# Turning blocks of 128x128 by fp32 products with the identity instead of transpose mode, in the samples' attention and the first two query tiles

## What is computed

```python
# compressed, selected and window branch, each a softmax over its keys
s = jnp.einsum('btghd,bkgd->bghtk', q, k) * scale + bias
p = jax.nn.softmax(jnp.where(ok, s, NEG), axis=-1)
o = jnp.einsum('bghtk,bkgd->btghd', p, v)
# merged by sigmoid gates, multiplied by the gate path, then projected
y = concat([o_merged * silu(z_nsa), u * mix * silu(z_g)]) @ w_out
```

## Time and profile before

| what | value |
|---|---|
| median of 3 runs | 1179.73 us (1175.66 to 1183.05) |
| the profiled execution | 1175.34 us, its span 1173.6 us |
| mean granted TensorE clock | 0.96 |
| PE busy | 1081.7 us (92%) |
| DVE busy | 587.2 us (50%) |
| ACT busy | 442.8 us (38%) |

### The profile page before, as it was taken

The page is one execution under the profiler, slowest core; times in us unless marked ns, Lnnn a source line. Parts: engine busy times, 40 slices in busy tenths (PEclk is TensorE's granted clock), DMA queues, the critical chain, the costliest instruction groups (busy, mean ns, idle before and its releaser), DMA issues. The chain is left out here.

```text
span 1173.6 us, 15483 instructions
## 1 busy us (share of the span) xinstructions
PE 1081.7 (92%) x6041; PEld 936.9 (80%) x6041; DVE 587.2 (50%) x1093; ACT 442.8 (38%) x746; POOL 191.0 (16%) x259
## 2 busy tenths in 40 slices
PE   6999999999998788889888789999899999998996
PEld 5879879999996676777777676887788889996884
DVE  4534221133233577777877436344689995215322
ACT  4330121110034466676666403222276675214211
POOL 2210578000003232221100000001021220000110
PEclk9999999999997899999999956999999999998999
DMA  8451002121122000000010711222311111401221
GB/s 286 129 192 59 19 5 59 37 54 37 37 78 101 1 1 1 1 1 1 1 48 26 238 50 55 93 90 91 95 36 37 37 36 51 165 1 59 87 93 63
DMA packets 64566, 74.81 MB, mean 64 GB/s; under 512 B 13794, under 2 KB 48658, under 8 KB 64495
## 3 DMA queue, kind: packets, MB, share of 16 engines
q1 hardware_dynamic: 61902, 70.77, 19.0%
q0 software_dynamic: 2496, 3.04, 0.8%
q10 hardware_dynamic: 96, 0.03, 0.0%
HBM read 62.19 MB, written 16.34 MB: 67 GB/s over the span
## 5 line engine op out<-in xcount | busy, mean ns | idle before, releaser
L1301 PE MATMUL ps<-h1T_hi,w_c_hl 128*128 128x352 f32 x768 | 150.0, 325 | 12.9 <-ACT region_w L1244 8.7
L1301 PE MATMUL ps<-hT_hi,w_fm_hl 128*128 128x352 f32 x768 | 145.5, 324 | 0.8 <-ACT region_w L1093 0.8
L1301 PEld LDWEIGHTS ps<-h1T_hi,w_c_hl 128*128 128x128 f32 x768 | 128.0, 188 | 17.7 <-ACT region_w L1244 13.2
L1305 PE MATMUL ps<-ident,region_w 128*128 128x128 f32 (+2 forms) x730 | 116.9, 289 | 27.0 <-ACT region_w L1143 17.6
L1305 PEld LDWEIGHTS ps<-ident,region_w 128*128 128x128 f32 (+2 forms) x730 | 94.1, 149 | 53.1 <-DVE p_hl L2008 23.8
L1301 PEld LDWEIGHTS ps<-hT_hi,w_fm_hl 128*128 128x128 f32 x768 | 127.4, 188 | 1.3 <-issue 1.2
L2008 DVE TENSOR_TENSOR p_hl<-ps,p_hl 128x512 fp32r<-128x512 f32 x132 | 91.2, 691 | 72.9 <-ACT p_hl L1151 71.1
L1151 ACT CAST p_hl<-ps 128x512 fp32r<-128x512 f32 x132 | 77.2, 585 | 73.5 <-PE ps L1305 73.1
L1301 PE MATMUL ps<-p_hl,v_hl 128*128 128x512 f32 x264 | 95.4, 443 | 6.7 <-DVE p_hl L2008 3.4
L1143 ACT ACTIVATE region_w<-region_w,negm 128x640 f32<-128x640 f32 (+7 forms) x128 | 93.8, 735 | 5.5 <-DVE negm L1983 4.5
L1983 DVE CUSTOM_DVE_ANT_0 region_w<-ps,region_w 128x640 f32<-128x640 f32 (+7 forms) x128 | 88.0, 699 | 5.1 <-PE ps L1301 4.7
(11 more groups left out here) (278 smaller groups left out, 1823.1 us busy)
## 6 DMA issues: line engine op xcount, KB each, us to landing
region_w<-in_x_prompt SPq DMA_DIRECT2D x16, 512.0 KB, 3.6
region_w<-in_w_in_c SPq DMA_DIRECT2D x16, 512.0 KB, 3.9
region_w<-in_w_in_a SPq DMA_DIRECT2D x12, 512.0 KB, 3.8
rel_rows_dram<-rel_line_dram SPq DMA_DIRECT2D x8, 576.0 KB, 12.5
region_y<-in_w_in_a SPq DMA_DIRECT2D x8, 512.0 KB, 6.2
region_w<-rel_rows_dram SPq DMA_DIRECT2D x16, 256.0 KB, 4.8
region_w<-in_w_out_a SPq DMA_DIRECT2D x2, 2048.0 KB, 12.1
x_dram<-region_w SPq DMA_DIRECT2D x8, 512.0 KB, 2.6
```

The costliest lines, as they stand in the source:

```text
L1301: return nc.tensor.matmul(out, l, r, start=start, stop=stop, skip_group_check=True)
L1305: return nc.tensor.transpose(out, x, ident[0:k, 0:k])
```

## The change

A second helper turns a block by an ordinary fp32 product: the block is the stationary operand, as before, and the identity streams through. It takes the place of `flip` in all turns of the samples' keys, window keys and probabilities, and in the `turn` steps of query tiles 0 and 1. `turn_result`, `c_turn`, `out` and the turns of tiles 2 to 7 stay as they are. No instruction changes its place, no wait and no buffer changes.

```diff
+PRODUCT_TILES = 2
...
+            def turn_by_product(out, x):
+
+                k = x.shape[0]
+                return mm(out, x, ident[0:k, 0:k], True, True)
...
                     for c in range(HPG):
-                        m = flip(ps[:, 4 + k % 3, c * P:(c + 1) * P], probs[kind][:, c, b * P:(b + 1) * P])
+                        m = (turn_by_product if i < PRODUCT_TILES else flip)(
+                            ps[:, 4 + k % 3, c * P:(c + 1) * P], probs[kind][:, c, b * P:(b + 1) * P])
...
                 for j in range(2 * HALF):
-                    m = flip(ps[:, bank + j // 4, (j % 4) * P:(j % 4 + 1) * P], h.pages[:, j, 256:384])
+                    m = turn_by_product(ps[:, bank + j // 4, (j % 4) * P:(j % 4 + 1) * P], h.pages[:, j, 256:384])
...
                 for j in range(2 * HALF):
-                    flip(ps[:, bank + 2 + j // 4, (j % 4) * P:(j % 4 + 1) * P], h.wins[:, j, 0:P])
+                    turn_by_product(ps[:, bank + 2 + j // 4, (j % 4) * P:(j % 4 + 1) * P], h.wins[:, j, 0:P])
...
-                    flip(ps[:, bank + 1 + b, 0:P], buf[:, 0:P])
-                    flip(ps[:, bank + 1 + b, P:2 * P], buf[:, P:2 * P])
-                    flip(ps[0:NS, bank + 1 + b, 2 * P:3 * P], buf[:, PAST:PAST + NS])
-                return flip(ps[0:16, bank + 3, 0:P], h.logits_c)
+                    turn_by_product(ps[:, bank + 1 + b, 0:P], buf[:, 0:P])
+                    turn_by_product(ps[:, bank + 1 + b, P:2 * P], buf[:, P:2 * P])
+                    turn_by_product(ps[0:NS, bank + 1 + b, 2 * P:3 * P], buf[:, PAST:PAST + NS])
+                return turn_by_product(ps[0:16, bank + 3, 0:P], h.logits_c)
```

## The result

The changed kernel takes 1185.6 us in the median of 18 runs (1182.3 to 1190.97), the kernel before 1176.75 us in 18 runs (1170.74 to 1184.34). The ratio is 1.0073, with a 95% interval of 1.0054 to 1.0091: slower by 8.6 us (6.4 to 10.7). Forecast were 8.1 us more.

A forecast was written before the change was run, and what follows sets the result against it. PE bounds the samples but for one wait, and a ring of PE, ACT and DVE the tiles. Tiles +3.8 and samples +4.3 sum to +8.1 us, from 1179.73 to 1187.8; range 1174 to 1197.

The forecast's parts named there:

- The bound from the averages: Samples' averages, only 2 columns wide, take 0.42 us a product at 1.2 GHz: lower bound for the new product's price.
- Tiles: Turns of query tiles 0 and 1: +6.6 us on the path less 2.8 from the clock, +3.8 (bounds -2 to +9).
- the ring: In tiles 0 and 1 PE turns, ACT casts, DVE subtracts, PE waits 0.93 us; a later turn delays everything.
- the rise 7 us sooner: In tiles 0 and 1 the clock's rise at 384.3 comes some 7 us earlier, saving at most 2.8 us.
- Samples: Samples' attention: +7.3 us of longer turns on PE's path less 3.0 from the clock, +4.3 (bounds -8 to +10).
- first turns: The samples' first 24 turns, begun at the low clock level, end later as products: +2.9 us.
- the other eight: The samples' eight turns of the other half, with the clock falling or fallen: 3.3 us for 1.5, +1.5.
- The 14 products of the probabilities: Turns of the samples' probabilities at the low clock level: 14 x 0.21 = +2.9 us.
- The saving of 3 us in the values: Samples' value products partly run at 2.4 GHz after the probabilities' turns raise the clock: 3 of 8 us saved.
- The clock stays up: Rival: from first pages to output products, products keep or wake the high clock; about -15 us, 1164.5; chance 0.10.
- Nothing given back: Rival: in tiles and samples the clock does what it does now; +13.9 us, 1193.6; chance 0.25.
- Mostly hidden: Rival: more of the tiles' turn groups covered by PE's idle time; about +4 us, 1183.7; chance 0.15.

The follow-up runs named there:

- Measured alone: Against the kernel before, products only in the turns of query tiles 0 and 1, samples keeping transpositions: 1.0029, +3.4 us.
- all tiles: The change with products in the turns of all eight query tiles instead of two: 1.04, +47 us against the kernel before.
- samples alone: Against the kernel before, products only in the samples' attention, tiles keeping transpositions: 1.0016, +1.9 us.
- order: The change with each half's wide products of the probabilities made first and the narrow ones behind: 1.0055, +6.5 us against the kernel before.
- turned twice by transposition: The change with each of its 94 products replaced by two transpositions into the same place: 1.0033, +3.9 us against the kernel before.
- a gap filled by transpositions: The kernel before with 18 unused identity transpositions in PE's wait for the samples' exponentials: 0.9982.
- one filled by products: The kernel before with 9 unused fp32 identity products in PE's wait for the samples' exponentials: 0.9973.
- four fills together: The kernel before with PE's waits filled in four places by work with unused results: 0.9909, 1165.98 us.

## Why the prediction was right

The forecast was a price of +13.9 us, 5.8 of it given back by the clock, and so +8.1. Measured are +8.6; by the line through the runs of the kernel before, 12.4 of price and 3.7 given back (0.961 for 0.957). The mechanism holds: a product costs twice a transposition, most of that lies on the path, and a part comes back through the clock. Its level, 1187.8, was 2.2 us too high, since the median of the three runs it started from (1179.73) lies 3.0 us over that of the 18.

**The price of a product.** Foreseen 0.225 us at 2.4 GHz and 0.43 at 1.2 GHz; measured 0.20 and 0.425. The bound from the averages (0.42) was the right neighbour.

**Tiles.** Forecast +6.6 on the path less 2.8 of clock, +3.8. Measured alone +3.4 (0.7 to 6.2); at equal mean clock +6.6. That ACT's cast follows each turn was right: the ring got longer, and with all tiles four fifths of the price or more showed. By the forecast's own mark, the way to the first turn of tile 2, the change's profile grew by 8.4 us and not by 4, and the first low stretch got longer (23.9 us for 20.7) where it was to end sooner. About 5 of the 8.4 are price; the rest is 10 us more at the low level (37.5 for 27.3). So the rise 7 us sooner isn't how the clock gave something back in that execution. It came in one of six profiles with longer turns, and where in the tiles the runs gain their higher mean clock no profile shows.

**Samples.** Forecast +4.3; the profiled stage grew by 5.5, of which 0.4 came back in the first output; alone the part measured +1.9 (-1.1 to 4.9), and +7.7 at equal mean clock, where +7.3 was forecast without the clock. By terms: first turns +2.6 for +2.9, the other eight +1.7 for +1.5. The 14 products of the probabilities cost +4.5 and not +2.9, since in a product each change between a wide and a narrow stationary operand costs 0.45 us, which in a transposition it hardly does. The forecast had only the length of the records in this term. The saving of 3 us in the values had the right size and an uncertain place: it came there in "samples alone" (5.9 us for 9.2), in "order" and in "all tiles" (5.8 each); in the change's profile 2.9 us came at the second averages in its place, because the clock rose there.

**The rivals.** "The clock stays up" rested on a difference between the modes. The Trainium skill (TensorE: Matmul & The Clock Gate, Part 4: PE-mode transpose) says that the full clock doesn't engage for transpose mode, which doesn't count as busy time in the same way. That isn't borne out here for fp32 turns: turned twice by transposition the clock rose within 4.6 us of turns, and a gap filled by transpositions gave the same 2.4 GHz behind it as one filled by products (706.74 and 706.91). "Nothing given back", +13.9, is outside the measured interval. "Mostly hidden", about +4, is too, and the kernel with all tiles contradicts it. The total was near with help from errors that cancel, and that part is luck: the probabilities' price was 1.6 us too low, the tiles' clock came otherwise than told, and the prices of the two parts alone (6.6 and 7.7) add up to more than the whole's 12.4.

Still open: what decides when in an execution the clock changes. With it the way to tile 2 moves from 60.9 to 67.3 us for the same turns. I also didn't settle whether the stops at the width switches keep the clock low through the probabilities. For it: with fewer stops it rose during them, and the runs have a higher mean clock (0.964 for 0.961). Against it: with the same stops it rose at their end in "samples alone" and during them in "all tiles", where the 28 records took 6.5 us.

## What to carry to other kernels

Turning a block by an fp32 product costs twice a transposition at either clock, and no run here shows it to buy anything for the clock that transpositions of the same length don't. When the clock is low behind a wait, fill the wait itself with work whose result nobody reads, as long as it ends before the wait does: that costs nothing on the path, and here took 0.9% off with four fills together. Keep operands of one width together in a run of fp32 products. Before reading a difference of two profiles stage by stage, compare their mean clocks with those of the other runs: here the profile of the change was the slowest of 18, and nearly half of its +15.6 us was the clock.

## What the runs showed of the hardware that was not expected

- In fp32 products, alternating stationary operands of 128 and of 32 or 16 columns costs 0.45 us for each excursion at 1.2 GHz (1.73 us for six records instead of 1.28); grouping the widths took 0.45 off the half (3.87 to 3.42). Transpositions of the same widths kept 0.227 us each, where wide ones alone take 0.214.
- Work on the identity, with a result that is constant, raises the clock like real work: 18 records were put into 4.1 us of a 4.2 us gap from 699.4 on, and the clock rose near 704.8 and not at 722.2.
- The place of a clock change differs between executions of the same instructions. It moved a stage of 47 us by up to 3.6 with transpositions and one of 51 us by up to 6.6 with longer turns.
- Most of the spread between runs of one kernel goes with the clock: the kernel before took 1184.67 us at a mean granted clock of 0.952 and 1169.28 at 0.967.
